# Sums of a tile turned in ring banks chosen at the drain, and tokens of even tiles turned at the end of the last tile's dots

## The reference

```python
q = (h @ wq).reshape(B, L, 8, 2, 128)                 # 8 heads
s1, s2 = q[..., 0, :] @ k1.T, q[..., 1, :] @ k2.T      # 128 keys each
# top 16 of each, top 16 of their 256 sums -> 16 experts for each head: 128 picks for each token
a   = einsum('cd,ckd->ck', hx, u_tab[e])               # the dots
out = einsum('ck,ckd->cd', g * gelu(a), v_tab[e])      # the weighted sums
x   = x + out
```

## Time and profile before

| what | value |
|---|---|
| median of 3 runs | 3542.54 us (3542.4 to 3544.26) |
| profiled execution, its time | 3546.33 us |
| profiled execution, its span | 3544.5 us |
| busy share of the span | PE 85%, DVE 77%, ACT 30%, POOL 30% |
| moved by DMA | 1299.16 MB, mean 367 GB/s |

### The profile page before, as it was taken

One profiled execution on the slowest core, in us unless ns is written; L12 is line 12 of the kernel. 1 busy time (PEld: TensorE's weight loads), 2 busy tenths in 40 slices (PEclk: granted clock), 3 DMA queues, 4 the chain that ended last, 5 costly groups with the idle time before them and its releaser, 6 DMA issues.

```text
span 3544.5 us, 37294 instructions
## 1 busy us (share of the span) xinstructions
PE 3030.0 (85%) x11036; PEld 1952.5 (55%) x11036; DVE 2715.3 (77%) x6651; ACT 1061.7 (30%) x2433; POOL 1048.3 (30%) x1090
## 2 busy tenths in 40 slices
PE   8999989889999689788998679888998777777775
PEld 7788766456766356355775347445776422223222
DVE  6575698987668798889767888888867989855555
ACT  2341143334322143343322233333421233221111
POOL 1010023332223332333223333333223333333332
PEclk9999999999999789989999889999999989999997
DMA  4335589999999999999999999999999999999997
GB/s 175 119 125 207 203 345 410 413 405 361 403 406 412 375 370 418 406 398 376 408 400 406 398 367 417 412 398 385 395 409 404 391 370 421 421 419 381 420 421 288
DMA packets 214343, 1299.16 MB, mean 367 GB/s; under 512 B 23872, under 2 KB 28352, under 8 KB 82944
## 3 DMA queue, kind: packets, MB, share of 16 engines
q0 software_dynamic: 151504, 1087.72, 75.8%
q1 hardware_dynamic: 62640, 209.06, 15.3%
HBM read 1282.01 MB, written 14.68 MB: 366 GB/s over the span
## 4 chain that ended last, share of the span: by engine, by line
PE 49%; DMA 23%; DVE 20%; issue 5%; ACT 3%; POOL 0%; DVEq 0%; ACTq 0%; POOLq 0%
DMA heap<-table_uv,heap 23%; PE ps L952 22%; PE ps L1182 17%; DVE heap L2143 8%; PE ps L1119 4%; DVE heap L1838 2%; PE ps L1012 2%; ACT heap L1462 1%; PE ps L1063 1%; PE ps L1069 1%; PE ps L1103 1%; DVE temp L2009 1%; PE ps L1081 0%; PE ps L993 0%; DVE rms L1953 0%
## 5 line engine op out<-in xcount | busy, mean ns | idle before, releaser
L1182 PE MATMUL ps<-heap 128*128 128x512 f32 x2792 | 1446.2, 653 | 436.9 <-ACT heap L1462 418.3
L923 POOL DMA_INDIRECT heap<-table_uv,heap x1024 | 1012.4, 989 | 2158.1 <-PE ps L1182 1778.7
L2143 DVE CUSTOM_DVE_ANT_0 heap<-heap,ps 128x1024 f32<-128x1024 f32 x1016 | 1233.8, 1217 | 382.4 <-DMA heap<-table_uv,heap 379.5
L1182 PEld LDWEIGHTS ps<-heap 128*128 128x128 f32 x2792 | 533.5, 202 | 1143.1 <-ACT heap L1462 668.4
L952 PE MATMUL ps<-hT,ring 128*128 128x256 f32 x3840 | 875.8, 383 | 11.3 <-DVE hT L1957 6.3
L952 PEld LDWEIGHTS ps<-hT,ring 128*128 128x128 f32 x3840 | 736.1, 193 | 169.7 <-issue 69.7
L1480 ACT ACTIVATE heap<-heap 128x2 f32<-128x2 f32 x512 | 104.0, 203 | 1505.5 <-DVE heap L2143 1503.1
L1838 DVE SCALAR_TENSOR_TENSOR heap<-heap 128x1024 f32<-128x1024 f32 x319 | 408.1, 1279 | 4.0 <-DVE xT L2066 2.9
L1462 ACT ACTIVATE heap<-ident,heap 128x128 f32<-128x128 f32 x698 | 267.9, 391 | 169.9 <-DVE heap L2154 164.0
L2154 DVE SCALAR_TENSOR_TENSOR heap<-heap 128x2 f32<-128x2 f32 x512 | 111.1, 217 | 182.1 <-ACT heap L1480 175.3
L1480 ACT ACT_TABLE_LOAD x122 | 156.5, 1283 | 5.4
(11 more groups left out here) (270 smaller groups left out, 2518.1 us busy)
## 6 DMA issues: line engine op xcount, KB each, us to landing
ring<-weights SPq DMA_DIRECT2D x344, 512.0 KB, 8.5
ring<-ssm_par SPq DMA_DIRECT2D x36, 512.0 KB, 11.9
heap<-table_uv,heap POOLq DMA_INDIRECT x1024, 9.8
ssm_par<-heap POOLq DMA_DIRECT2D x20, 512.0 KB, 5.1
ring<-weights SPq DMA_DIRECT2D x20, 256.0 KB, 7.8
ssm_par<-heap POOLq DMA_DIRECT2D x8, 256.0 KB, 3.9
xT<-x_cm SPq DMA_DIRECT2D x2, 512.0 KB, 5.0
heap<-ssm_bc POOLq DMA_DIRECT2D x2, 512.0 KB, 8.8
```

Of the source, the lines that this page charges most:

```text
L923: pool.indirect_dma_start(rows[:, j, :], None, table_uv, bass.IndirectOffsetOnAxis(expert[:, tile % 2, k:k + 1], 0)).then_inc(row_landed[j ...
L1182: mm = pe.matmul(ps[:, SUM_BANK + half, :], diag[:, PE_TURN[v] % DIAGS, :], rows[:, v % NR, D + half * 512:D + (half + 1) * 512], start=(k ...
L2143: dve.tensor_tensor_reduce(row, row, token, 1.0, 0.0, ALU.mult, ALU.add, act_st[:, g % WIDE, pick % GROUP:pick % GROUP + 1]).then_inc(dott ...
```

## The change

The PE part and the second DVE part of `drain` become items of their own, `home`, one for each half of a tile. A `home` turns four blocks of `tile_sum` in a bank of the ring, DVE adds that bank to `xT`, and frees it. The planner places the two `home` items of a tile between two mixer items as soon as the drain is planned, so that the order of the ring's units now comes out of the plan. The first PE sum of the next tile waits for the drain's adds alone (`sum_joined`); the first DVE sum waits for the second `home`'s transposes.

The `htok` of even tiles leaves the written order. The planner places it three picks ahead of the end of the last tile's dots (for stage 0 behind the score of the first head), and its ACT copies go ahead of ACT's other work once these dots are planned. The `htok` of odd tiles is no longer held back.

The last norm uses one fixed bank of the ring (`FINAL_BANK`) for its three parts, and `home` units planned after the mixer's end use the other three.

```diff
-    return out + [("htok", u, t, half) for t in range(2) for half in range(2)]
+    return out + [("htok", u, 1, half) for half in range(2)]
...
-    "ptab": ("DVE",), "tb": ("PE", "ACT"), "wt": ("PE", "ACT", "DVE"), "drain": ("DVE", "PE", "DVE"),
+    "ptab": ("DVE",), "tb": ("PE", "ACT"), "wt": ("PE", "ACT", "DVE"), "drain": ("DVE",), "home": ("PE", "DVE"),
...
     if kind == "squares":
-        return [end("drain", 2 * u - 4 + i) for i in range(2)] if u >= 2 else []
+        home = [end("home", 2 * u - 4 + i, half) for i in range(2) for half in range(2)] if u >= 2 else []
+        return home + ([end("htok", u - 1, t, 1) for t in range(2)] if u else [])
...
+def bank_of(n):
+
+    if n < LAST:
+        return n % (8 if n < EARLY else 4)
+    return (FINAL_BANK + 1 + (n - LAST) % 3) % 4
...
-        if v < u and (v % PICKS or v == 0 or (("drain", v // PICKS - 1), 2) in done) and v // GROUP * GROUP + GROUP <= u and (v // GROUP * GROUP + GROUP - 1) in end_of \
+        if v < u and (v % PICKS or v == 0 or (("drain", v // PICKS - 1), 0) in done) and v // GROUP * GROUP + GROUP <= u and (v // GROUP * GROUP + GROUP - 1) in end_of \
...
-            tile_open = v < PICKS or ready([(("drain", v // PICKS - 1), 1)], s)
+            tile_open = v < PICKS or ready([(("home", v // PICKS - 1, 1), 0)], s)
...
-        while at < len(order) and pe > 0:
+        while pe > 0:
+            if left is None:
+                for stage in waiting_tokens:
+                    if ready([(("score", 0, 0), 0)], s) if stage == 0 else u >= 2 * stage * PICKS - 3 and ready([(("mean", stage, 1), 2)], s):
+                        waiting_tokens.remove(stage)
+                        order[at:at] = [("htok", stage, 0, half) for half in range(2)]
+                    break
+                if homes and ready([(("drain", homes[0]), 0)], s):
+                    order[at:at] = [("home", homes[0], half) for half in range(2)]
+                    homes.popleft()
+            if at == len(order):
+                break
             item = order[at]
-            if item[0] == "htok" and item[1] and u < 2 * item[1] * PICKS:
-                break
...
+        if queue["TOKENS"]:
+            first = 2 * queue["TOKENS"][0][0][1] * PICKS
+            if first == 0 or u >= first and end_of[first - 1] < s:
+                act = run("TOKENS", 100.0, s, slot["ACT"])
         run("ACT", act, s, slot["ACT"])
...
-                if kind == "drain":
-                    tile = item[1]
-                    pe.wait_ge(sum_joined, 2 * (tile + 1))
-                    for c in range(8):
-                        mm = pe.transpose(ps[:, SUM_BANK + c // 4, (c % 4) * P:(c % 4 + 1) * P],
-                                          tile_sum[:, c * P:(c + 1) * P], ident[:])
-                        yield
-                    mm.then_inc(sum_turned, 1)
-                    return
...
+                elif kind == "home":
+                    _, tile, half = item
+                    pe.wait_ge(sum_joined, 2 * (tile + 1))
+                    for c in range(4):
+                        mm = pe.transpose(ps[:, b, c * P:(c + 1) * P], tile_sum[:, half * 512 + c * P:half * 512 + (c + 1) * P], ident[:])
+                        if c == 3:
+                            end(mm)
+                        yield
...
                 if k == 0 and tile:
-                    pe.wait_ge(x_home, 2 * tile)
+                    pe.wait_ge(sum_joined, 2 * tile)
...
                     if tile:
-                        dve.wait_ge(sum_turned, tile)
+                        dve.wait_ge(tiles_done, UNIT[("home", tile - 1, 1)] + 1)
...
+                elif kind == "home":
+                    _, tile, half = item
+                    b, t0 = done_unit(item), (tile % NT) * P
+                    dst = xT[:, 4 * half:4 * half + 4, t0:t0 + P]
+                    dve.tensor_tensor(dst, dst, ps[:, b, :].rearrange("p (k c) -> p k c", k=4), ALU.add).then_inc(x_home, 1)
+                    dve.wait_ge(x_home, 2 * tile + half + 1)
+                    dve.sem_inc(bank_free[b], 1)
+                    yield
```

More of the change, by code:

```diff
@@ L191, in weight_of @@
                 "branch": (8 if item[-1] < 2 else 4, .43) if kind == "branch" else 0, "score": (4, .28), "htok": (4, .2),
-                "tb": (4, .2), "wt": (16, .28), "masks": (2, .3), "drain": (8, .2), "final": (8, .4)}.get(kind, (16, .43))
+                "tb": (4, .2), "wt": (16, .28), "masks": (2, .3), "home": (4, .2), "final": (8, .4)}.get(kind, (16, .43))
     if eng == "ACT":
@@ L200, in weight_of @@
             "pb": (44, .2), "pd": (8, .6), "ptb": (18, .55), "pca": (24, .55), "ptab": (75, .3), "wt": (4, .29),
-            "drain": (2, .7), "final": (9, .5)}.get(kind, (1, .3))
+            "drain": (2, .7), "home": (1, .7), "final": (9, .5)}.get(kind, (1, .3))
 def final_part(kind):
@@ L212, in prior @@
     if kind == "squares":
-        return [end("drain", 2 * u - 4 + i) for i in range(2)] if u >= 2 else []
+        home = [end("home", 2 * u - 4 + i, half) for i in range(2) for half in range(2)] if u >= 2 else []
+        return home + ([end("htok", u - 1, t, 1) for t in range(2)] if u else [])
+    if kind == "home":
+        return [end("drain", u)]
     if kind == "final":
-        return [end("htok", STAGES - 1, 1, 1)] + ([end("final", u - 1)] if u else [])
+        return [end("htok", STAGES - 1, t, 1) for t in range(2)] + ([end("final", u - 1)] if u else [])
     if kind == "mean":
@@ L375, in piece_list @@
     out, at = [], {}
-    for item in RING_UNITS:
+    for item in PLACED:
         for name in pieces_of(item):
             at[(item[1], name)] = len(out)
-            out.append((item[1], name, UNIT[item]))
+            out.append((item[1], name, item))
     return out, at
 PIECE_LIST, PIECE_AT = piece_list()
-MIX_END = {u: UNIT[("mix", u, 1)] for u in range(STAGES)}
 def ring_holders(item):
@@ L410, in make_plan @@
     slots, done = [], {}
-    queue = {"ACT": deque(), "DVE": deque(), "SPIN": deque(), "TOP": deque(), "PREP": deque(), "DRAIN": deque()}
-    order, at, left = ORDER, 0, None
+    queue = {"ACT": deque(), "DVE": deque(), "SPIN": deque(), "TOP": deque(), "PREP": deque(), "DRAIN": deque(),
+             "TOKENS": deque()}
+    order, at, left, units = list(ORDER), 0, None, []
+    homes, waiting_tokens = deque(range(TILES)), deque(range(STAGES))
     u = v = 0
@@ L433, in enqueue @@
             return
-        if eng == "DVE" and item[0] == "drain":
+        if eng == "DVE" and item[0] in ("drain", "home"):
             eng = "DRAIN"
+        elif eng == "ACT" and item[0] == "htok" and item[2] == 0:
+            eng = "TOKENS"
         elif eng == "DVE" and item[0] in ("top", "settle"):
@@ L467, in make_plan @@
     s = 0
-    while at < len(order) or v < TILES * PICKS or any(queue.values()) or shut or finals:
+    while at < len(order) or v < TILES * PICKS or any(queue.values()) or shut or finals or homes:
         slot = {"u": None, "v": None, "PE": [], "ACT": [], "DVE": []}
@@ L491, in make_plan @@
             tokens += 2
-        while finals and ready([(("drain", FINALS[finals[0]][0]), 2)] + prior(("final", finals[0])), s):
+        while finals and ready([(("home", FINALS[finals[0]][0], half), 1) for half in range(2)] + prior(("final", finals[0])), s):
             enqueue(("final", finals.popleft()), 0, s)
@@ L514, in make_plan @@
                     break
-                if item in UNIT and bank_before(UNIT[item]) is not None:
-                    if not ready([bank_holder(bank_before(UNIT[item]))], s):
+                if item[0] in RINGED:
+                    before = bank_before(len(units))
+                    if before is not None and not ready([bank_holder(units[before])], s):
                         break
+                    units.append(item)
                 left = weight_of(item, 0)[0]
@@ L543, in make_plan @@
         assert s < 6000, (order[at] if at < len(order) else None, u, v, left, {k: list(q)[:2] for k, q in queue.items()})
-    return slots
-PLAN = make_plan()
+    return slots, units
+PLAN, RING_UNITS = make_plan()
+UNIT = {item: n for n, item in enumerate(RING_UNITS)}
+BANK = [bank_of(n) for n in range(len(RING_UNITS))]
+BANK_USES = [BANK[:n].count(BANK[n]) for n in range(len(RING_UNITS))]
+BANK_TOTAL = [BANK.count(b) for b in range(8)]
+MIX_END = {u: UNIT[("mix", u, 1)] for u in range(STAGES)}
 ON_DVE = [slot["v"] for slot in PLAN if slot["v"] is not None and slot["v_on"] == "DVE"]
@@ L1225, in emit @@
                     if u:
-                        act.wait_ge(tiles_done, UNIT[("htok", u - 1, 1, 1)] + 1)
+                        act.wait_ge(tiles_done, max(UNIT[("htok", u - 1, t, 1)] for t in range(2)) + 1)
                     yield from squares(u, norm_of(u, 0))
@@ new lines, in emit @@
+                    wait_summed(dve, PICKS * (tile + 1) - 1)
+                    mine = DVE_OF_TILE[tile]
+                    if mine:
+                        wait_summed(dve, mine[-1])
```

(11 more changed lines are left out.)

52 lines of the change are left out of this document (15 added, 37 removed).

## The result

The changed kernel takes 3433.16 us, the median of four runs (3429.1 to 3437.55), against 3542.47 for the kernel before (3533.72 to 3544.26, the three runs of the table above and one more). The ratio is 0.9696 with a 95% interval of 0.9676 to 0.9717: 109 us, or 3.0%, faster. Forecast were 3496.5 us and a range of 3465 to 3530. So the direction was right and the gain was more than twice what the sum gave. The profiled execution took 3429.1 us, its span is 3426.9.

The account below looks back on a forecast made before the run. From the first picks on, the 1,024 gathers of 1 MB (DMA) set the pace, PE and DVE close behind. 20 + 26 + 3 - 3 = 46 us off the profiled 3546.3, against the median 3496.5 us; range 3465 to 3530.

Parts of the forecast that it names:

- memory already sets the mean rate: Rival: gaps fill but the stretches between slow as much, or gaps shift elsewhere; no change, 3542.5 us; chance 0.05.
- all idle DMA time comes back: Rival: start 29, boundaries 42.6 and dots 5, so 77 us off, 3465.5 us; chance 0.10.
- the next tile's sums wait for the join: At the seven drains of tiles 0 to 6: sums no longer wait for the way home; 26 us, bounds 18.0 and 42.6.
- The start: Tile 0's tokens behind the first head's scores, first dot at 403 for 447.08; 20 us, between nothing and 29.
- the engines would swallow it: Rival: the early start of tile 0 is worth nothing, 3516.5 us; chance 0.12.
- The tokens of the other even tiles: Tokens of tiles 2, 4 and 6 turned early, next dots sooner; 3 us, between nothing and 15.6.
- the slower rival: Rival: the mixer becomes late, so tile 2 waits for its first settle; 3565.5 us; chance 0.10.
- the adds: Sixteen times DVE waits for its own add before freeing the bank; costs 3 us, up to 10.

Follow-up runs that it names:

- the way home alone: Changed kernel without the early start and without the early tokens of tiles 2, 4 and 6; 3468.52 us, ratio 0.9802.
- the limit alone: Kernel before with LAG 3 in place of 4, so dots run at most three picks ahead of the sums; 3498.13 us, ratio 0.9888.
- pause with and without it: Changed kernel with first sums of odd tiles planned two slots later: with LAG 4, 3476.1 us, ratio 0.9834; with LAG 3, 3441.24 us, ratio 0.972.
- the old distance in after: Changed kernel with the first sums of odd tiles planned two slots later, LAG 4, so sums stand four picks back; 3476.1 us, ratio 0.9834.
- the kernel before at the shorter distance: Kernel before with tile 0's tokens behind the first head's scores and LAG 3; 3459.04 us, ratio 0.9768.
- the longer one: Kernel before with tile 0's tokens behind the first head's scores, LAG still 4; 3511.04 us, ratio 0.9909.
- after without the early start: Changed kernel with tile 0's tokens placed behind the last head's scores; 3467.34 us, ratio 0.981.

## Why the prediction was right in sign and wrong in size

**What held.** The DMA's idle time was what could be won, and the change won it: the rate inside the stretches did not fall as the gaps closed (419 GB/s beside picks alone, from 2790 to 3070, as before). The rival by which memory already sets the mean rate is gone. The one in which all idle DMA time comes back (3465.5) was nearest, and still too slow, since it counted that time only where the stops were seen. The Trainium skill, "Perfetto Trace Analysis", section "Engine Utilization", says that the 358 GB/s are a core's share when both cores of a pair use the memory, and that a single active core can pull more, up to about 435 GB/s of its 16 DMA engines; the trace, with 418 GB/s from 420 to 470 and 411 through tile 1, agrees.

**The step that failed: "the next tile's sums wait for the join".** The prediction priced this edit by the stop at the drain: 29.5 read directly, 26 taken, and 42.6 as the bound from above, "all that the DMA lost" in 15 us behind each drain. The stop itself was sized well: 22 us in the seven windows, 18 to 30 in the run with the way home alone against the limit alone. But the bound was none, because the loss did not end after 15 us. The stop shifts sums against dots in the plan's lists, and that shift stays for 128 picks. I had read `LAG` in the code and took it for a limit; it was the state in which tiles 1, 3 and 5 ran. It cost 39 us (limit alone), 35 to 40 (pause with and without it). The place to see it was in the trace of before, in rows that weren't asked for: tiles 1, 3 and 5 were 26 to 39 us longer than their even neighbours 2 and 4 (after the change 11 to 22 us are left, so not all of that was the distance), and the dots of tile 1 waited 71.3 us for gathers. Tile 2's, asked in the same way for 1257 to 1637, waited

```profile
DVE heap L2143 <- DMA heap<-table_uv,heap: 12.1, 14, 2.4
```

Why a pick more matters can be worked out from the trace: from the start of a dot to the issue of the next gather into its row, tile 1 takes 16.4 us on average over its 128 picks before, 11.6 after, 12.3 with the limit at three, 15.5 with the old distance in after. The DMA, with fewer gathers in flight, lands each one sooner, and still moves less in all. The issues from each tile-1 window (before, then after; median us to landing):

```profile
heap<-table_uv,heap POOLq DMA_INDIRECT x122, 9.2
```

```profile
heap<-table_uv,heap POOLq DMA_INDIRECT x123, 11.1
```

The Trainium skill, "Perfetto Trace Analysis", section "Optimization Strategy", names this reading: the same gap repeating through a stretch can mean that there are too few buffers for the next tile. Seven rows for eight, 46 us slower, agree.

**The start was taken at 20 and bounded by 29; the runs give 34 to 41** after, 42 in the kernel before at the shorter distance, and 32 there at the longer one. The first dot runs at 401.01 (403 was forecast), 46.1 us earlier. Tile 0 takes 10.6 us longer for it, the price of the other heads' queries that now share its engines, so 35.5 arrive at its end. The fear that the engines would swallow it did not come true: from 420 to 470 the lost 29 us came back in full. The traces of after and of after without the early start differ by 33.6 us, 30.1 of them at tile 0's last dot (789.62 for 819.76). So the bound of 29 was about right, and what the ratios give beyond it is hardly more than their interval, some 11 us. The mis-sized step was the 20, by which a third of that idle time should have been lost to the queries.

**The tokens of the other even tiles**, taken at 3, give nothing alone and some 9 beside the early start, hardly told from nothing. The gap ahead of tile 2 stays at 7.9 us, where under 5 was forecast; those ahead of tiles 4 and 6 are 4.2 and 4.7. Ahead of tile 2 the copies are done at 1192.23, and DVE then works off top-16s until the dot at 1195.69, without a pause:

```profile
1187.81 1.21 DVE L2172 CUSTOM_DVE_ANT_0 heap<-heap,ps 128x1024 f32<-128x1024 f32 x1
...
1194.90 0.42 DVE L1933 FIND_INDEX8 heap<-heap 128x8 uint32<-128x256 f32 x1
1195.35 0.43 DVE L1936 MAX8 heap<-heap 128x8 f32<-128x256 f32 x1
1195.69 1.20 DVE L2172 CUSTOM_DVE_ANT_0 heap<-heap,ps 128x1024 f32<-128x1024 f32 x1
```

**What should have shown.** A PE sum ran 0.15 us behind the join's end in six of the seven drains, and 1.4 us behind it at tile 1's. Gathers 7 us apart at most: not at the drains of tiles 2, 5 and 6, with some 8.5 us each. Windows at 320 GB/s: five of seven. Stage 1's squares ran at 484.9, inside 480 to 540. Tile 2's first settle was through at 1143, 53 us ahead of its first dot, so the slower rival, which needed squares behind 597, never came near. POOL's wait behind the eighth gather is 8.12 us, for 52.56, and no `home` shows a wait for a ring bank.

**The sum as it should have been**: start 30 to 41, distance 39, pauses 18 to 30, tokens 0 to 9, less whatever the adds cost, which no run shows. That is 87 to 119, with 109 measured. The upper figures of start, pauses and tokens are differences from runs of the changed kernel itself, so this is an account of the 109 us and no test of it.

## What to carry to other kernels

Where engines follow a fixed order, a stop at one point isn't over when it ends: it leaves one list shifted against another, and the shift stays until something makes the leading list wait. So price it over the whole stretch that it shifts, by the time that a buffer is held, and compare stretches with like work (here odd tiles with even ones) before the gaps between them. The best distance between a producer and its consumer lies between holding buffers too long and waiting for each other; here one pick cost 39 us on the one side and 19 on the other.

## What the runs showed of the hardware

The median time of a 1 MB gather from issue to landing, in tile 1, was 9.2 us at 392 GB/s (before), 10.2 at 401 (limit at three) and 11.1 at 411 (after); with the old distance in after it was 9.3, also at 401. So the order by rate isn't strict, but a longer landing time was here no sign of a slower DMA: it went with rows that were freed sooner (11.6 and 12.3 us from a dot to the next gather into its row, against 15.5 and 16.4), and so with gathers that were issued sooner.

The granted clock in tile 1 was 0.93 before and 0.99 after, where 1.00 is all of it at 2.4 GHz and PE was busier in the second. The clock isn't what made the 39 us of the distance, as the limit alone gave its 39 us at 0.93. What a higher clock gave to the rest of the change no run sets apart: over the whole run it was 0.94 before and 0.96 after, and a PE matrix multiplication of the sums took 633 ns on average for 653.
